# Two fused blocks on one core: where the last expert's weights lie, when the surplus tile runs, and how the second block's vector work is ordered

## What is computed

```python
def hierarchical_moe(x, ...):                  # block 1, its last part: 32 experts
    combine = ...                              # per token: two experts of one group of eight
    for g in range(N_GROUPS):
        h = silu(einsum('nd,edf->nef', xt, w_gate[g])) * einsum('nd,edf->nef', xt, w_up[g])
        out = out + einsum('nef,efd->nd', h * combine[:, g, :, None], w_down[g])
def second_block(x, ...):
    h = rms_norm(x, g_mix[l])
    z = einsum("bsd,de->bse", h, w_in[l]) + b_in[l]          # 7168 columns
    va, ga, xb, gb, sa, sb = split(z, ...)                   # 1024, 1024, 1536, 1536, 1024, 1024
    u = causal_depthwise_conv(va * sigmoid(ga), conv_a_w[l], conv_a_b[l])     # 31 taps
    y_a = silu(layer_norm(u, ln_g[l], ln_b[l])) @ w_a_out[l]
    v = rg_lru(causal_depthwise_conv(xb, ...), ...)          # 4 taps, two gates, a linear scan
    y_b = (v * gelu(gb)) @ w_b_out[l]
    x = x + (sigmoid(sa) * y_a + sigmoid(sb) * y_b) @ w_o[l]
    ...                                                      # then an MLP of width 4096
```

## Time and profile before

| | us |
|---|---|
| median of 3 runs | 1114.71 |
| lowest, highest | 1113.94, 1118.01 |
| the profiled execution | 1114.88 |
| its span, first to last instruction | 1113.1 |
| PE busy in the span | 889.3 (80%) |
| DVE, ACT, POOL busy | 530.1, 360.0, 204.6 |

### The profile page before, as it was taken

How to read it: one execution, slowest core, us unless ns; L and a number is a source line. 1 busy time by engine, 2 the same in 40 slices (tenths; PEclk the granted TensorE clock), 3 DMA queues, 4 the chain that set the end, 5 groups by cost and what they waited for, 6 DMA issues and landing times.

```text
span 1113.1 us, 17939 instructions
## 1 busy us (share of the span) xinstructions
PE 889.3 (80%) x7803; PEld 724.2 (65%) x7803; DVE 530.1 (48%) x832; ACT 360.0 (32%) x473; POOL 204.6 (18%) x90
## 2 busy tenths in 40 slices
PE   7987868656464747565687699998999989999997
PEld 6986865323242424233353599588899988988986
DVE  4553554202121212121222789999984756644542
ACT  5624212101010101010111544466466345524441
POOL 1041400000000000000000978404039920000000
...
GB/s 345 263 266 1 312 142 333 429 426 429 427 430 427 430 427 429 428 428 429 428 426 385 70 176 182 76 116 148 151 183 264 197 151 152 168 210 169 208 78 38
DMA packets 83794, 299.90 MB, mean 269 GB/s; under 512 B 9197, under 2 KB 47645, under 8 KB 71453
## 3 DMA queue, kind: packets, MB, share of 16 engines
...
q10 hardware_dynamic: 144, 0.00, 0.0%
...
## 4 chain that ended last, share of the span: by engine, by line
PE 56%; DMA 29%; DVE 9%; ACT 3%; issue 2%; SPq 1%; DVEq 0%; ACTq 0%
DMA mem<-in_w_up 26%; PE PS L1693 12%; PE PS L1694 12%; PE PS L1695 12%; PE PS L1868 8%; PE PS L1877 3%; DVE PS L1494 2%; DMA mem<-in_w_in 2%; PE PS L2050 1%; PE PS L1856 1%; PE PS L2053 1%; DVE mem L1604 1%; DMA mem<-in_w 1%; PE PS L1890 1%; DVE ring_rest L1472 1%
## 5 line engine op out<-in xcount | busy, mean ns | idle before, releaser
L1868 PE MATMUL PS<-mem 128*32 128x256 f32 x2048 | 157.8, 476 | 127.2 <-DMA mem<-in_w_up 127.1
L1868 PEld LDWEIGHTS PS<-mem 128*32 128x32 f32 x2048 | 84.6, 136 | 202.2 <-issue 180.8
L1695 PE MATMUL PS<-HT_hi,ring_rest 128*128 128x256 f32 x752 | 214.2, 285 | 0.0
L1695 PEld LDWEIGHTS PS<-HT_hi,ring_rest 128*128 128x128 f32 x752 | 145.4, 193 | 0.0
L1693 PE MATMUL PS<-HT_hi,z_hi 128*128 128x256 f32 x440 | 126.8, 288 | 7.6 <-ACT mem L889 5.6
L1288 DVE TENSOR_TENSOR mem<-mem,PS 128x128 f32<-128x128 f32 x32 | 12.2, 380 | 253.3 <-ACT mem L794 253.3
L1694 PE MATMUL PS<-HT_rest,z_hi 128*128 128x256 f32 x440 | 126.1, 287 | 0.0
L622 POOL TENSOR_TENSOR ring_rest<-mem,z_hi 128x2048 fp32r<-128x2048 f32 x19 | 88.3, 4657 | 102.4 <-DVE ring_rest L1472 83.9
L1611 DVE TENSOR_TENSOR ring_rest<-mem,mlp_hi 128x4096 fp32r<-128x4096 f32 x16 | 70.8, 4424 | 57.9 <-ACT mlp_hi L988 57.9
L627 POOL TENSOR_TENSOR ring_rest<-mem,z_hi 128x512 fp32r<-128x512 f32 x4 | 5.9, 1518 | 479.6 <-ACT z_hi L816 479.6
L1693 PEld LDWEIGHTS PS<-HT_hi,z_hi 128*128 128x128 f32 x440 | 86.0, 196 | 9.0 <-ACT mem L889 8.1
...
## 6 DMA issues: line engine op xcount, KB each, us to landing
...
```

The lines of the kernel that those rows point to most:

```text
L1695: ins = nc.tensor.matmul(dst, s_rest, m_hi, start=False, stop=stop and n == len(terms) - 1, skip_group_check=True)
L1868: ins = nc.tensor.matmul(PS[SLOTS * j:SLOTS * (j + 1), bank, 0:2 * F_STRIP].rearrange("p (w n) -> p w n", w=2), xg[:, k, :], w[:, :, k, F_ ...
```

## The change

- **Surplus tile.** It runs in pack 1 instead of pack 7 (`OVER_PACK`). Packs 0, 1 and 7 are written out on every engine and packs 2 to 6 are the loop; pack 7 has no `If` left in it.
- **Last expert.** Gate, up and down of expert 31 go into the third slots, which are free by then. SP issues gate and up of 31 directly behind those of 30, and down of 31 directly behind that of 30, in two halves; PE's down of 31 waits for each half apart.
- **Gathers.** The two rounds go into two PSUM banks (7 and 6), so that the second round waits for nothing of the first.
- **Between the blocks.** ACT's table for the square root is loaded ahead of the last expert's collection; DVE hands over its small sums tile by tile; POOL's rest of the first z block waits until the norm's rows are written; PE's first chunk begins on the high part alone (`first_times_hT`).
- **LRU.** The `bd` tables lie where ga and gb will stand, are cleared by POOL earlier, and are loaded by SP (18 transfers) behind the first four z blocks instead of by POOL (12). PE's gate matmuls wait for a bank less. The exponentials stand half behind block 13 and half behind block 14, the roots behind 17 and 18; the four gb blocks taken meanwhile (14, 15, 18, 19) are taken plain, and a gelu over 4 chunks follows.
- **DVE.** The last pair's taps are cut: start and 20 taps, then the four scan rounds and the rest of h, then the last 10 taps, the sum, the rest of late unit 0 and only then the subtraction of the mean. On PE the mean's matmul comes behind the last round of z. ACT squares the centred values behind `split_late(1)`.

```diff
-OVER_AT = EXPERTS - PACK
+OVER_PACK = 1
+OVER_AT = OVER_PACK * PACK
...
-REST_LRU, REST_SCAN = (16, 17, 18), (22, 23, 24, 25)
+REST_LRU, REST_SCAN = (16, 17, 18), (23, 24, 25, 26)
...
-ACT_ROOT, ACT_H = 17, 23
+ACT_EXP, ACT_ROOT, ACT_H = 13, 17, 23
+GB_PLAIN = (ACT_EXP + 1, ACT_EXP + 2, ACT_ROOT + 1, ACT_ROOT + 2)
...
 WO_TURN = 6
-ACT_CENTRED = 25
+TAPS_FIRST = 21
 MASKED = -1e30
 
-B_COMB, B_GATE, B_DOWN, B_GATHER = 0, 2, 4, 7
+B_COMB, B_GATE, B_DOWN, B_GATHER, B_SECOND = 0, 2, 4, 7, 6
...
+        BDX = gate_table(gb_place[:, 0:BD], RG)
+        BDA_most, BDA_last = gate_table(ga_place[:, 0:BD // RG * 3], 3), gate_table(gb_place[:, BD:BD + BD // RG], 1)
...
-            return PS[:, 3 * (g % 2) + q // 2, (q % 2) * T:(q % 2 + 1) * T]
+            return PS[:, ((B_SHORT, B_SHORT + 1, 0), (1, 2, 3))[g % 2][q // 2], (q % 2) * T:(q % 2 + 1) * T]
...
-            with sp.Fori(2, OVER_AT // 2) as pair:
-                load_pair(pair)
+            load_pair(2)
...
+                    sp.wait_ge(down_done, THIRD_EXPERT + 1)
                     load_over(0)
...
+            with sp.If(n_extra > 1):
+                with sp.Fori(1, EXTRA_MAX) as j:
+                    with sp.If(j < n_extra):
+                        sp.wait_ge(over_down_done, j)
+                        load_over(j)
+            with sp.Fori(4, EXPERTS // 2 - 1) as pair:
                 load_pair(pair)
+            last = EXPERTS - 1
+            sp.wait_ge(gu_done, last - 2)
+            load_gate_up(last - 1, first)
+            load_expert(last, [p for p, _ in third[0:2]], [last_loaded, last_loaded])
+            sp.wait_ge(down_done, last - 2)
+            load_down(last - 1, *first[2])
+            for half in range(2):
+                at = slice(half * SLOT_FLOATS // 2, (half + 1) * SLOT_FLOATS // 2)
+                sp.dma_start(third[2][0][:, at], wd_d[last][:, at]).then_inc(last_down[half], 16)
...
+            sp.wait_ge(pads_ready, 1)
+            for bd, w, g0, g1 in ((BDX, A["w_rg_x_2"], 0, RG), (BDA_most, A["w_rg_a_2"], 0, 3), (BDA_last, A["w_rg_a_2"], 3, RG)):
...
+                        sp.dma_start(bd[r0 - chunk * P:r1 - chunk * P, :, chunk, c0:c0 + RNN_HEAD],
+                                     heads[h, r0 - h * RNN_HEAD:r1 - h * RNN_HEAD, g0:g1]).then_inc(bd_loaded, 16)
...
+            pool.wait_ge(gu_done, EXPERTS - 2)
+            link(nc.gpsimd.memset(ga_place, 0.0))
+            nc.gpsimd.memset(gb_place, 0.0).then_inc(pads_ready, 1)
+            pool.wait_ge(rows, rows_before["mix2"] + TT)
             pool.wait_ge(z_hi_ready, 1)
...
                 ins = nc.gpsimd.tensor_tensor(z_rest(0)[:, at], z_raw(0)[:, at], z_hi(0)[:, at].bitcast(F32), ALU.subtract)
             ins.then_inc(z_rest_ready, 1)
...
+                if i == PACK - 1:
+                    act.preload_act_table_set(SQRT_SET)
+                collect(e + i, i)
+                if i + 2 < PACK:
+                    gate(e + i + 2, i + 2)
+
             split_half(0)
-            act.preload_act_table_set(SQRT_SET)
...
-                    act.wait_ge(mix2_in, 1)
+                act.wait_ge(mix2_in, tt + 1)
...
-                    func = (ACT.Identity if ch < C_GA or C_XB <= ch < C_GB else
+                    func = (ACT.Identity if ch < C_GA or C_XB <= ch < C_GB or n in GB_PLAIN else
...
+            def gelu_plain(first):
+                chunk = 2 * IN2_ORDER[first] - C_GA
+                act.wait_ge(z_bank_free, Z_BANKS + 2 * (first + 2))
+                gb = Z[:, chunk:chunk + 4, :]
+                nc.scalar.activation(gb, gb, ACT.Gelu_apprx_tanh).then_inc(gb_ready, 1)
...
+                if n == ACT_H:
+                    split_h()
                 if n + HI < IN2_HALVES:
...
-                if n == LRU_AFTER * IN2_GROUP + 1:
-                    lru_exponentials()
-                if n == ACT_ROOT:
-                    lru_roots()
...
+                for i in range(2):
+                    if n == ACT_EXP + i:
+                        lru_exponentials(range(2 * i, 2 * i + 2))
+                    if n == ACT_ROOT + i:
+                        lru_roots(range(2 * i, 2 * i + 2))
+                if n in (ACT_EXP + 2, ACT_ROOT + 2):
+                    gelu_plain(n - 1)
...
             split_late(1)
+            act.wait_ge(centred, 1)
+            nc.scalar.activation(Z[:, Z_GA:Z_GA + KC, :], CU, ACT.Square).then_inc(sq_ready, 1)
...
-                for r in range(2):
+                for r, bank in enumerate((B_GATHER, B_SECOND)):
                     dve.wait_ge(gath_ps, 2 * pack + (r + 1))
                     ks = slice(4 * r, 4 * r + 4)
-                    nc.vector.tensor_tensor(XG[:, ks, :], PS[:, B_GATHER, :].rearrange("p (k s) -> p k s", k=4),
...
-            conv_a(3)
-            for i in range(2):
-                dve.wait_ge(tap_step[i], TAPS_A * KC // 2)
-            nc.vector.tensor_reduce(Z[:, Z_GA, :], CU.rearrange("p k t -> p t k"), AX_X, ALU.add).then_inc(sum_ready, 1)
-
+            conv_a_start(3)
+            conv_a_taps(3, range(1, TAPS_FIRST))
             for g in range(RG):
...
+                    dve.wait_ge(gb_ready, 2)
                 nc.vector.tensor_tensor(RB[:, rows_, :], RB[:, rows_, :], Z[:, Z_GB + 3 * g:Z_GB + 3 * g + 3, :], ALU.mult).then_inc(h_ready, 1)
...
-            dve.wait_ge(mean_ps, 1)
-            nc.vector.tensor_tensor(CU, CU, PS[:, 4, 0:T].unsqueeze(1).broadcast_to((P, KC, T)), ALU.subtract).then_inc(centred, 1)
...
+            conv_a_taps(3, range(TAPS_FIRST, TAPS_A))
+            for i in range(2):
+                dve.wait_ge(tap_step[i], TAPS_A * KC // 2)
+            nc.vector.tensor_reduce(Z[:, Z_GA, :], CU.rearrange("p k t -> p t k"), AX_X, ALU.add).then_inc(sum_ready, 1)
...
             dve.wait_ge(late_hi_ready, LATE_DVE + 1)
             nc.vector.tensor_tensor(rest, raw, hi.bitcast(F32), ALU.subtract).then_inc(late_rest_dve, 1)
+            dve.wait_ge(mean_ps, 1)
+            nc.vector.tensor_tensor(CU, CU, PS[:, 4, 0:T].unsqueeze(1).broadcast_to((P, KC, T)), ALU.subtract).then_inc(centred, 1)
...
-                for r in range(2):
-                    pe.wait_ge(xg_ready, 2 * pack + r)
+                pe.wait_ge(xg_ready, 2 * pack)
+                for r, bank in enumerate((B_GATHER, B_SECOND)):
                     for k in range(4):
                         for tt in range(TT):
-                            ins = nc.tensor.matmul(PS[:, B_GATHER, k * P:(k + 1) * P], HN[:, tt, 4 * r + k, :], sel[:, tt, :],
+                            ins = nc.tensor.matmul(PS[:, bank, k * P:(k + 1) * P], HN[:, tt, 4 * r + k, :], sel[:, tt, :],
...
-                pe.wait_ge(xg_ready, 2 * pack + 2)
+                pe.wait_ge(xg_ready, 2 * pack + 1)
...
+                    if halves and k % 2 == 0:
+                        pe.wait_ge(halves[k // 2], 16)
...
+            with pe.Fori(OVER_PACK + 1, PACKS - 1) as pack:
+                expert_pack(pack)
+            expert_gate_up(PACKS - 1, 0)
...
+                if i + 1 < PACK - 1:
+                    expert_gate_up(PACKS - 1, i + 1)
+                else:
+                    pe.wait_ge(last_loaded, 32)
+                    gate_up(third_at, B_GATE + (PACK - 1) % 2, XG[:, :, SLOTS * (PACK - 1):], gu_done)
+                expert_down(PACKS - 1, i)
+            pe.wait_ge(hidT_ready, EXPERTS)
+            down(third_at + 2 * SLOT_FLOATS, B_DOWN + (PACK - 1) % 2, hidT[:, (PACK - 1) % 2, :], down_done, last_down)
...
                     nc.tensor.matmul(by_token_tile(dst), hi[:, k, cols], HT_hi[:, :, k, :], start=k == 0, stop=False, skip_group_check=True)
+                pe.wait_ge(rest_ready, rest_count)
+                for k in range(KC):
...
-                    pe.wait_ge(z_rest_ready, IN2_GROUP * r + (h + 1))
+                    if isinstance(r, int) and (r, h) == (0, 0):
+                        pe.wait_ge(z_hi_ready, 1)
+                    else:
+                        pe.wait_ge(z_rest_ready, IN2_GROUP * r + (h + 1))
...
-                        if 2 * h + i == 3 and after_lru:
+                        if 2 * h + i == 1 and after_lru:
                             pe.wait_ge(lru_gates, RG)
...
-                    pe.wait_ge(z_bank_free, Z_BANKS + 2 * IN2_GROUP * LRU_AFTER - 1 + g)
+                    pe.wait_ge(z_bank_free, Z_BANKS + 2 * IN2_GROUP * LRU_AFTER - (3 if g == 0 else 0))
...
                 z_round(r, True)
+            z_round(IN2_HALVES // IN2_GROUP - 1, True)
             pe.wait_ge(sum_ready, 1)
             nc.tensor.matmul(PS[:, 4, 0:T], mean_ones[:, :], Z[:, Z_GA, :], start=True, stop=True).then_inc(mean_ps, 1)
-            z_round(IN2_HALVES // IN2_GROUP - 1, True)
```

153 lines of the change are left out of this document (81 added, 72 removed).

## The result

| | before | changed |
|---|---|---|
| median, us | 1115.07 (4 runs) | 1104.48 (4 runs) |
| lowest, highest | 1113.94, 1118.01 | 1100.26, 1109.08 |
| profiled execution: span | 1113.1 | 1107.6 |

The ratio is 0.9892, 95% interval 0.9861 to 0.9923: 10.6 us faster. The forecast was 1108, with 1098 to 1114 as range: sign and range were right, the size was 3.6 us short, and of the two ways out of the fork the trace took the one that was forecast.

The account below looks back on a forecast made before the run. The experts' two ends, PE's waits in the second block and half clock behind pauses were taken as bounding; -1.1 - 4.3 - 0.6 - 0.5 + 1.6 - 1.9 = -6.8 gave about 1108 us, range 1098 to 1114.

Parts of the forecast that it names:

- the fork: Before y, POOL (821.7) or DVE (822.0) subtracts its late rest first, holding the other up; POOL first was forecast.
- What bounds the kernel: The experts' stage is worth its two ends, as weight loads run at 429 GB/s; then PE's waits and half clock.
- Gathers: Pack 0 at the experts' start: second gather round no longer waits for the first read; -1.1 us, bounds -0.7 and -1.5.
- The last expert: End of the experts: combination starts sooner after the last down load lands; -4.3 us, bounds -3.5 (half clock) and -6.
- Between the blocks: Norm before z: DVE's products without POOL's subtraction save 2.0, PE waiting for POOL costs 1.4; net -0.6 us.
- z: PE's waits for ACT and DVE and the half clock behind them go; z ends at 817.9 instead of 830.8.
- DVE becomes the bound: From last LRU rest to sum DVE needs 63.3 us; y starts at 832.0 against 832.5, -0.5, giving back nearly all z gains.
- The stand: PE idle between the end of z and y, waiting for DVE's sum and late rest; forecast at 14.1 us.
- Clock and w_o: Half clock at the start of y costs +1.6 us; PE's shorter wait for DVE at w_o gives -1.9.
- A: Rival before y: DVE goes first, y starts 6.5 us earlier; 1101.5, down to 1098; chance 0.27.
- B: Rival: gains swallowed by the w_o wait, clock and waiting for POOL between the blocks; 1111 to 1112.5; chance 0.20 with D.
- C: Rival in the straight last pack: engines stop for instructions, 5 us each; one gives 1113, two or more 1118; chance 0.06.

Follow-up runs that it names:

- DVE first: Changed kernel with one wait more: POOL's rest of late unit 1 waits for DVE's rest of late unit 0; 1101.55 us, ratio 0.9861 to before.
- POOL first: Changed kernel with one wait more: DVE's rest of late unit 0 waits for POOL's rest of late unit 1; 1103.81 us, ratio 0.9891 to before.
- the rest of h last: On top of DVE first, DVE's last ten taps and the sum moved ahead of the rest of h's four subtractions; 1092.83 us, ratio 0.9796 to before.

## Why the prediction was right, and where it was off

- **What bounds the kernel.** Right. Both ends of the experts' stage, not its middle, moved the time, and the surplus tile's detour in pack 1 starved no transfer.
- **Gathers.** -1.9 for -1.1, beyond the bound of -1.5. The read (0.8 with its gaps) was counted; left out were PE's own time (6.68 us for both rounds, where before it took 3.80 and 3.67) and the two matmuls of L1861 (0.4), which now run beside DVE's last read.
- **The last expert.** -3.6 for -4.3, but the combination then takes 1.8 longer. The bound of half clock was seen for the down (1.8, measured 1.98), not for the combination that follows it at once. Taken apart, the gathers' 2.5 reach the last byte, the tile's removal alone adds 1.1 behind it and the third slots 3.2, half of that lost to the clock; the medians don't separate the last two.
- **Between the blocks.** The term that failed: -0.6, measured -4.2. The step was to count POOL's subtraction as what holds DVE up and to leave out POOL's clearing, which stood beside the norm. The first is worth nothing on balance (the +1.4 that I set against the -2.0 was about right), the second 3.2 to 3.6.
- **z.** 13.4 us shorter for 12.9 (the prediction's own terms add up to an end at 818.1, not 817.9, so 12.7; by that POOL's lead at the fork would have been 0.1 and not 0.3). The mechanism was right for ACT's waits, but plain takes and not the cut in two bring most of it. The cut of the taps brings 7.4 inside z, not the 1.9 of one wait: taken back alone, it costs 5.1 and half clock, and none of it reaches the kernel's time.
- **DVE becomes the bound.** The best step. From the last LRU rest to the sum DVE takes 63.5 us (forecast 63.3); 1.0 of it is a wait for ACT's gelu over four chunks, where the prediction had 1.3 for POOL. The stand was forecast at 14.1 and measured at 13.9; of the 13.4 us that PE gains in z, 12.2 are given back. POOL was to begin 0.3 ahead of DVE and began 0.54 ahead. Rows and runs agree with the exclusive lock that the Trainium skill ("SBUF - State Buffer", section "Who interferes with whom") states: 9.33 is POOL's remainder plus DVE's own time, not a shared rate, and the order alone moves y by 5.6.
- **Clock and w_o.** +1.6 for y came as 3.2 us at 0.50. At w_o the wait fell by 1.1, and the clock stayed full behind it, where in before 6.5 us at half clock followed: -4.4 in place of -1.9. This is luck in part: behind waits hardly shorter (1.11 and 0.96 with DVE first) the clock fell to half for over 3 us, and y to w_o took 88.3 to 88.6 us in the traces with DVE first, POOL first and the rest of h last, against 86.1 and 85.3 in the two of the changed kernel.
- **The rivals.** A needs DVE first, which didn't happen in either trace; made to happen it gives 1101.55, as A had it (1101.5), but by two errors that cancel: the fork is worth 5.6 in the trace and some 3 in the time, not 6.5, and the rest of the change brings more than forecast. B did not come. C: no piece without a releaser of over 3 us stands in the straight last pack.

The sum of the terms was -6.8 and the traces give -11.9 without the two chance rows. The 5.1 between them: gathers -0.8, the last load +0.7 and the combination's half clock +1.8, between the blocks -3.6, z -0.5, the stand -0.2, y to w_o -2.5. Of these the combination's +1.8 and w_o's -2.5 come and go between executions, so the forecast's error that belongs to the change is mostly the -3.6 between the blocks and the -0.8 of the gathers.
